# Compressed branch's first layer: keys and values in the two column halves of the array, in two parts

## The reference, cut to what matters

```
def compress(k, pe, w1, w2):              # k: 512 tokens, 2 groups of 64; once for keys, once for values
    blocks = ... windows of 32 tokens, stride 16: n_cmp = 31
    flat = (blocks + pe) as (31 * 2 groups, 32 * 64 = 2048)
    return gelu(flat @ w1) @ w2           # w1: 2048 x 256, w2: 256 x 64
k_cmp = compress(kc, pe_k, w_ck1, w_ck2)
v_cmp = compress(vc, pe_v, w_cv1, w_cv2)
```

## Time and profile before

| | us |
|---|---|
| median of 3 runs (1547.8 to 1548.92) | 1548.38 |
| the profiled execution, its own time | 1548.38 |
| its span | 1546.6 |
| TensorE matmul busy (share) | 1509.5 (98%) |
| VectorE busy | 890.8 (58%) |
| ScalarE busy | 767.9 (50%) |
| GpSimd busy | 726.3 (47%) |
| mean granted TensorE clock | 0.996 |

### The profile page before, as it was taken

One profiled execution on the slowest core, in us unless ns is written; L12 is line 12 of the kernel. 1 busy time (PEld: TensorE's weight loads), 2 busy tenths in 40 slices (PEclk: granted clock), 3 DMA queues, 4 the chain that ended last, 5 costly groups with the idle time before them and its releaser, 6 DMA issues.

```text
span 1546.6 us, 19684 instructions
## 1 busy us (share of the span) xinstructions
PE 1509.5 (98%) x7349; PEld 1186.3 (77%) x7349; DVE 890.8 (58%) x1450; ACT 767.9 (50%) x1227; POOL 726.3 (47%) x462
## 2 busy tenths in 40 slices
PE   7999999999999999999999999999999899999997
PEld 6776556888888888888887777777888578888885
DVE  5358895233143784847535423531002699999998
ACT  5377876223244323232244644632224378888885
POOL 4266666435584646555454654744447163111100
PEclk9999999999999999999999999999999999999999
DMA  7430001422224465455232331222236299999984
GB/s 258 143 103 15 1 1 42 144 95 95 97 101 144 175 233 192 178 204 188 86 100 68 110 123 42 69 69 68 96 103 268 83 388 381 401 382 383 380 300 178
DMA packets 74942, 250.79 MB, mean 162 GB/s; under 512 B 11731, under 2 KB 13075, under 8 KB 74840
## 3 DMA queue, kind: packets, MB, share of 16 engines
q1 hardware_dynamic: 67264, 234.41, 42.0%
q0 software_dynamic: 4752, 8.11, 1.4%
q10 hardware_dynamic: 2824, 6.94, 1.2%
HBM read 244.94 MB, written 12.66 MB: 167 GB/s over the span
## 4 chain that ended last, share of the span: by engine, by line
PE 90%; DVE 5%; ACT 2%; DMA 1%; issue 1%; SPq 1%; POOL 1%; DVEq 0%; ACTq 0%
PE ps L432 17%; PE ps L436 17%; PE ps L433 17%; PE ps L999 4%; PE ps L1003 4%; PE ps L1000 4%; PE ps L455 2%; PE ps L1032 2%; PE ps L458 2%; PE ps L461 2%; PE ps L1028 2%; PE ps L1029 2%; PE ps L491 2%; PE ps L648 1%; PE ps L805 1%; PE ps L614 1%
## 5 line engine op out<-in xcount | busy, mean ns | idle before, releaser
L305 POOL TENSOR_TENSOR RS<-RAW,RS 128x1024 fp32r<-128x1024 f32 x173 | 432.2, 2502 | 406.9 <-ACT RS L300 400.0
L300 ACT ACTIVATE RS<-RAW 128x1024 fp32r<-128x1024 f32 x305 | 320.2, 1056 | 224.8 <-PE ps L436 134.0
L432 PE MATMUL ps<-RH,RS 128*128 128x512 f32 x808 | 320.0, 396 | 9.0 <-ACT RS L300 7.4
L436 PE MATMUL ps<-RH,RS 128*128 128x512 f32 x808 | 315.8, 391 | 0.6 <-POOL RS L305 0.6
L433 PE MATMUL ps<-RH,RS 128*128 128x512 f32 x808 | 315.3, 390 | 0.0
L432 PEld LDWEIGHTS ps<-RH,RS 128*128 128x128 f32 x808 | 152.3, 188 | 44.3 <-ACT RS L300 9.1
L436 PEld LDWEIGHTS ps<-RH,RS 128*128 128x128 f32 x808 | 152.1, 188 | 33.8 <-POOL RS L305 1.0
L433 PEld LDWEIGHTS ps<-RH,RS 128*128 128x128 f32 x808 | 152.4, 189 | 31.6 <-issue 1.0
L305 DVE TENSOR_TENSOR RS<-RAW,RS 128x1024 fp32r<-128x1024 f32 x132 | 154.8, 1218 | 8.7 <-ACT RS L300 8.5
L432 PE MATMUL ps<-RA,RS 128*128 128x512 f32 x400 | 156.3, 391 | 0.0
L433 PE MATMUL ps<-RA,RS 128*128 128x512 f32 x400 | 155.7, 389 | 0.0
(11 more groups left out here) (388 smaller groups left out, 2646.1 us busy)
## 6 DMA issues: line engine op xcount, KB each, us to landing
RAW<-in_w_ff SPq DMA_DIRECT2D x64, 512.0 KB, 4.6
RAW<-in_w_gate SPq DMA_DIRECT2D x46, 512.0 KB, 8.9
RAW<-in_w_up SPq DMA_DIRECT2D x43, 512.0 KB, 9.1
RAW<-in_w_down SPq DMA_DIRECT2D x41, 512.0 KB, 10.5
PB<-in_ada SPq DMA_DIRECT2D x24, 512.0 KB, 3.8
TB<-in_ada SPq DMA_DIRECT2D x24, 512.0 KB, 3.8
RAW<-in_w_gb SPq DMA_DIRECT2D x16, 512.0 KB, 3.2
RAW<-in_w_ga SPq DMA_DIRECT2D x16, 512.0 KB, 3.2
```

The source lines that it names most:

```text
L300: act.activation(RS[:, spl[n], 0, :], raws[slot[n]], ACT.Copy).then_inc(*HI.up(n))
L305: eng.tensor_tensor(RS[:, s, 1, :], raws[slot[n]], hif(RS[:, s, 0, :]), ALU.subtract).then_inc(*mark.up(n))
L432: pe.matmul(b[:, :], wh, xh, start=(k == 0), stop=False)
L436: last = pe.matmul(b[:, :], wl, xh, start=False, stop=(k == K - 1))
```

## The change

The plan puts chunks 0 and 1 of keys and of values behind the tile of place 6, and chunks 2 and 3 behind that of place 7, each chunk of the keys followed by the same chunk of the values. `compress_in` is called at both places with its chunks; it takes one bank, and for each piece it multiplies the keys into rows 0 to 61 and the values into rows 64 to 125. There is one semaphore step for a pair of chunks, and the Gelus write rows 0 to 61 and 64 to 125 of one tile, which is turned by two full transposes and copied out by one copy.

The splits that stand at chunks move with them. By the rules of the plan, w_qkv 0 now stands behind four raw chunks, so its split falls at chunk 0 (place 6) and no longer at place 4; its raw tile is loaded in its turn behind those four. Those of w_qkv 1, 2 and 3 stand at chunks 2 (keys), 2 (values) and 3 (keys), at place 7.

```diff
+CHUNKS = {6: (0, 1), 7: (2, 3)}
 ...
     for i, u in enumerate(QKV):
         plan.append(("w_qkv", u, "split"))
-        if i == 7:
-            whole("w_c", "raw")
+        if i in (6, 7):
+            plan.extend(("w_c", 4 * kv + c, "raw") for c in CHUNKS[i] for kv in (0, 1))
 ...
-    HIDS = [TB[:, 1, 0:256], TB[:, 1, 640:896]]
+    HID, HTF = TB[:, 1, 0:256], TB[:, 1, 256:512]
 ...
-        def compress_in():
-            for kv in range(2):
-                b = take(("ch", kv), B67)
-                pe.wait_ge(*V(("cmp", kv)))
-                for c in range(4):
-                    n = IDX["w_c", kv * 4 + c]
+        def compress_in(chunks):
+
+            if chunks[0] == 0:
+                take("ch", B67)
+                for kv in range(2):
+                    pe.wait_ge(*V(("cmp", kv)))
+            b = ps["ch"]
+            for c in chunks:
+                ns = [IDX["w_c", 4 * kv + c] for kv in range(2)]
+                for n in ns:
                     pe.wait_ge(*LANDED[slot[n]](n))
-                    for q in range(4):
-                        lp = 4 * c + q
-                        last = pe.matmul(b[0:62, 0:256], FP[kv][:, lp * 62:lp * 62 + 62],
-                                         raws[slot[n]][:, q * 256:q * 256 + 256], start=(lp == 0), stop=(lp == 15))
-                    last.then_inc(*P.up(("fed", n), ("ch", kv)))
+                for q in range(4):
+                    lp = 4 * c + q
+                    for kv in range(2):
+                        last = pe.matmul(b[64 * kv:64 * kv + 62, 0:256], FP[kv][:, lp * 62:lp * 62 + 62],
+                                         raws[slot[ns[kv]]][:, q * 256:q * 256 + 256], start=(lp == 0), stop=(lp == 15),
+                                         skip_group_check=True)
+                last.then_inc(*P.up(*(("fed", n) for n in ns), "ch"))
 
         def compress_turn():
-            for kv in range(2):
-                b = take(("ht", kv), B67)
-                pe.wait_ge(*A(("hid", kv)))
-                transposes(b, [(b[:, 128 * c:128 * c + 62], HIDS[kv][0:62, 128 * c:128 * c + 128]) for c in range(2)],
-                           ("ht", kv))
+            b = take("ht", B67)
+            pe.wait_ge(*A("hid"))
+            transposes(b, [(b[:, 128 * c:128 * c + 128], HID[:, 128 * c:128 * c + 128]) for c in range(2)], "ht")
 ...
             for f in FIN.get(i, ()):
                 fin(f)
-            if i == 7:
-                compress_in()
+            if i in CHUNKS:
+                compress_in(CHUNKS[i])
 ...
# ScalarE
             for f in FIN.get(i, ()):
                 fin(f)
+            if i in CHUNKS:
+                for c in CHUNKS[i]:
+                    for kv in range(2):
+                        splits_act(act, IDX["w_c", 4 * kv + c])
             if i == 7:
+                act.wait_ge(*V("scz2"))
                 for kv in range(2):
-                    for c in range(4):
-                        splits_act(act, IDX["w_c", 4 * kv + c])
-                    act.wait_ge(*V("scz2"))
-                    evict(("ch", kv), HIDS[kv][0:62, :], ACT.Gelu_apprx_tanh, slice(0, 62), slice(0, 256),
-                          [("hid", kv)])
+                    r = slice(64 * kv, 64 * kv + 62)
+                    evict("ch", HID[r, :], ACT.Gelu_apprx_tanh, r, slice(0, 256), ["hid"])
 ...
# VectorE
-            for kv in range(2):
-                dve.wait_ge(*P(("ht", kv)))
-                dve.tensor_copy(HT[kv], ps["ht", kv][:, 0:256].rearrange("p (c n) -> p c n", c=2)[:, :, 0:62]).then_inc(
-                    *V.up(("ev", ("ht", kv)), ("ht", kv)))
+            dve.wait_ge(*P("ht"))
+            dve.tensor_copy(HTF, ps["ht"][:, 0:256]).then_inc(*V.up(("ev", "ht")))
 ...
# GpSimd, and in the same way VectorE: the chunks' splits at places 6 and 7
             splits_pool(pool, IDX["w_qkv", u])
-            if i == 7:
-                for c in range(8):
-                    splits_pool(pool, IDX["w_c", c])
+            if i in CHUNKS:
+                for c in CHUNKS[i]:
+                    for kv in range(2):
+                        splits_pool(pool, IDX["w_c", 4 * kv + c])
```

More of the change, by code:

```diff
@@ L532, in fin @@
             pend[0] = u
-        def compress_in():
-            for kv in range(2):
-                b = take(("ch", kv), B67)
-                pe.wait_ge(*V(("cmp", kv)))
-                for c in range(4):
-                    n = IDX["w_c", kv * 4 + c]
-                    pe.wait_ge(*LANDED[slot[n]](n))
-                    for q in range(4):
-                        lp = 4 * c + q
-                        last = pe.matmul(b[0:62, 0:256], FP[kv][:, lp * 62:lp * 62 + 62],
-                                         raws[slot[n]][:, q * 256:q * 256 + 256], start=(lp == 0), stop=(lp == 15))
-                    last.then_inc(*P.up(("fed", n), ("ch", kv)))
-        def compress_turn():
-            for kv in range(2):
-                b = take(("ht", kv), B67)
-                pe.wait_ge(*A(("hid", kv)))
-                transposes(b, [(b[:, 128 * c:128 * c + 62], HIDS[kv][0:62, 128 * c:128 * c + 128]) for c in range(2)],
-                           ("ht", kv))
+        def compress_in(chunks):
[7 more added lines that the diff above has]
+                for n in ns:
+                    pe.wait_ge(*LANDED[slot[n]](n))
+                for q in range(4):
[5 more added lines that the diff above has]
+                last.then_inc(*P.up(*(("fed", n) for n in ns), "ch"))
+        def compress_turn():
+            b = take("ht", B67)
+            pe.wait_ge(*A("hid"))
+            transposes(b, [(b[:, 128 * c:128 * c + 128], HID[:, 128 * c:128 * c + 128]) for c in range(2)], "ht")
         def compress_out():
             b = take(("ck", 0), B67)
-            pe.wait_ge(*V(("ht", 0)))
+            pe.wait_ge(*V(("ev", "ht")))
             pe.wait_ge(*LD["cw2"](0))
@@ L561, in compress_out @@
             b = take(("ck", 1), B67)
-            pe.wait_ge(*V(("ht", 1)))
             for g in range(2):
@@ L1827, in vector @@
                 fin(f)
-            if i == 7:
-                for c in range(8):
-                    splits_dve(dve, IDX["w_c", c])
+            if i in CHUNKS:
+                for c in CHUNKS[i]:
+                    for kv in range(2):
+                        splits_dve(dve, IDX["w_c", 4 * kv + c])
             elif i == 8:
```

## The result

| | before | changed |
|---|---|---|
| median of 20 runs, us | 1549.45 (1547.71 to 1551.13) | 1552.18 (1550.31 to 1553.45) |
| profiled execution: time, span, us | 1548.38, 1546.6 | 1553.41, 1551.6 |
| its mean granted clock of TensorE | 0.996 | 0.991 |
| start of place 9's product, counted from the gates' transposes | 78.86 - 51.06 = 27.80 | 81.36 - 51.43 = 29.93 |

Changed against before: 1.0015, 95% interval 1.0009 to 1.0021, so some 2.3 us slower, inside the 0.2% that was called no change, and on its slower side. The forecast was 1550.4, 2.05 above its baseline of 1548.38, a median of three runs; that of the twenty runs here is 1.07 higher.

A forecast was written before the change was run, and what follows sets the result against it. TensorE was taken to bound the kernel, busy 1509.5 of 1546.6 us. Terms -7.0, -0.1, -0.6, +8.1 less 0.1, rounded to +0.25, plus 1.8 of low clock, onto 1548.38 gave 1550.4 us, range 1548.2 to 1552.7.

The forecast's parts named there:

- Part 1: Keys' and values' matmuls on TensorE overlap fully in two column halves: 3.5 us at each place, 7.0 us less in all.
- Part 3: Ahead of place 7's product, TensorE waits 6.0 and 1.9 us for w_qkv 0's split behind `fin`: stall of about 8.1 us.
- Part 4: After the wait, TensorE's clock falls to its low level for 4.0 us of place 7's product: 1.8 us lost.
- Part 5: Other moved splits, loads and Gelus cost nothing; at place 8 the Gelus are hidden by 0.2 us, so barely.
- the Gelu rival: Slow loads of w_qkv 2 and 3 delay the Gelus, TensorE waits 2.3 us at place 8's turning: 1552.7; chance 0.12.
- Turning: Ahead of place 9's product, two transposes instead of four: 0.38 to about 0.26 us, 0.1 less.
- Sum: Start of place 9's product and whole time: +0.25 + 1.8 = +2.05 us onto 1548.38, so 1550.4 us.
- The clock stays high: Rival: TensorE's gap ahead of place 7's product does not bring the low clock: +0.25, 1548.6; chance 0.13.
- The split is in time: Rival: ScalarE makes w_qkv 0's high half before TensorE wants it at 54.9: -7.6, 1540.8; chance 0.04.

The follow-up runs named there:

- same_half: Changed kernel with keys and values both into rows 0 to 61, beside each other in columns 0 to 255 and 256 to 511: 1555.08 us, 1.0041 of before.
- early_split: Changed kernel with w_qkv 0's halves made ahead of `fin` at place 6 on ScalarE and GpSimd: 1544.63 us, 0.9968 of before; repeats 1543.91 us.
- late_split: Kernel before with w_qkv 0's halves made behind `fin` of place 6 instead of at place 4: 1563.29 us, 1.0086 of before.
- kept_busy: Changed kernel with 26 added matmuls of 512 columns, result unused, behind the first half to fill TensorE's wait: 1550.20 us, 1.0005 of before.
- the second profile: Profile of the changed kernel run once more with nothing altered: 1552.68 us, 1.0018 of before.
- all_at_7: Changed kernel with all chunks at place 7, halves side by side, w_qkv 0 split at place 4 as before: 1549.99 us, 1.0006 of before.
- one_chunk: Changed kernel with chunk 0 alone at place 6 and chunks 1, 2 and 3 at place 7: 1546.17 us, 0.9986 of before.

## Why the prediction was right, step by step

- **Part 1.** 3.6 us at each place against 3.5. same_half gave the price of not doing it, 7.05. The Trainium skill (TensorE: Matmul & The Clock Gate, Part 3, The mechanism) lets weight loads overlap running matmuls only where the row group differs. The trace does not agree: the halves share their rows, their matmuls started 0.01 us apart at most, and weights were loaded at 51.86 and 51.87 while the matmuls of 51.81 ran.
- **Part 3.** The third matmul of place 7 came 63.97 - 51.43 = 12.54 us behind the gates' transposes; forecast 63.6 - 51.06 = 12.54. The idle times were 6.07 and 1.21 (6.0 and 1.9; at the low clock the two matmuls between fill more of the second). early_split and late_split show from both sides that the place of the split on ScalarE, behind `fin`, is the cause, and that the raw tile is none.
- **Part 4.** Place 7's other 22 matmuls took 7.20 us, forecast 5.13 + 1.8. The low level lasted until 68.18, 4.2 us of dense work; the middle taken was 4.0. kept_busy measured its price, 2.0, so the 1.8 was a little small. The Trainium skill (same page, HAM oscillation) says that idle gaps between bursts of matmuls throttle the engine again. The runs agree: the clock fell with the wait, in this kernel and in late_split; without the wait (early_split) it held at place 7.
- **Part 5.** No wait at place 8 for w_qkv 1, as said. The Gelus ended at 80.91 and TensorE asked for them at 81.2: hidden in the first profile, 0.31 us late in the second. "Hidden, but barely" is right, and the Gelu rival, 2.3 us, did not come: the loads of w_qkv 2 and 3, issued from 73.15, were there at 76.4 and 77.7, in 3.3 and 4.2 us, not 7.3.
- **Turning.** 1.01 us from place 8's end to place 9's start, against 1.35 before: 0.3 less, forecast 0.1. This small term was short.
- **Sum.** 29.93 - 27.80 = +2.13 at place 9, forecast +2.05; the second profile has +2.6. That the first is within 0.1 is in part luck: the clock cost 0.3 more than its term and the turning saved 0.2 more, and the two errors cancel. The medians say +2.7, the ratio 2.3. The time itself, 1552.18, lies 1.8 above the 1550.4 and over the 1551.5 from which the prediction counted "slower"; 1.07 of that is the low baseline of three runs, and the difference stays inside the 0.2%. What the forecast had no term for are the short stretches at the low clock near 130 and 840 us. The mean clocks say that before's runs have them as often, so they widen both kernels' spread; what brings them was not found.
- **Rivals.** "The clock stays high" was wrong by 2.0 us. "The split is in time" is the version that was then built: 6.1 us under before at place 9 and 5 to 5.6 in the medians, where 7.6 was given; it left out that w_qkv 1 would then be late (1.57).

## What to carry to other kernels

When splits, loads or other preparations are placed by a rule over a plan, moving a consumer in the plan moves them too: list, before and after, at which point of each in-order engine every preparation falls, and what stands ahead of it there. Work saved on the bounding engine in front of such a wait only lengthens the wait, and a long wait of TensorE costs a second time, in the clock of the matmuls behind it. A cheap test of the second price is to fill the wait with work that nobody uses.

## What the hardware showed that was not expected

- Two column halves are not kept in the order of the program matmul by matmul: with four pieces (eight records) of one half ahead of four of the other, the other half's first started at 52.54, ahead of the sixth record (52.75), and 32 records took 4.6 us, between the 3.6 of pairs and the 7.05 of one half.
- The clock fell behind shorter waits than the 3.34 us of the earlier trace rows: behind 2.62 and 1.70 us in same_half, and behind four waits of 0.3 to 1.8 us within 10 us in all_at_7. In one_chunk it held through 1.68, 0.37 and 1.70 us within 7 us.
- The mean clock of single runs of one kernel takes a few levels (0.996, 0.995 and 0.994 before), and from the first to the last they are worth some 2 us of its time. A change of 2 us is therefore as large as the spread, and was easier to read at one instruction of the profile than in the medians.
